# One product taken out of a mixing stage: second half of the conditioning, fetched by GpSimd in other stages

## What is computed

```python
mod = silu(c) @ w_ada + b_ada                       # (2048) x (2048, 6*2048)
sh1, sc1, g1, sh2, sc2, g2 = split(mod, 6)
u   = rms_norm(x) * (1 + sc1) + sh1
xa, ya, xb, xc, gl = split(u @ w_in)                # LRU, gelu gate, pool, Fourier, branch gates
lru_out  = ((h_f + h_b) * gelu(ya)) @ w_lru_out     # two scans over the tokens, gates from xa
pool_out = multiscale_pool(xb) @ w_pool * pool_scale
four_out = real(fft2(xc)) @ w_fourier
x = x + g1 * ((g_lru*lru_out + g_pool*pool_out + g_four*four_out) @ w_out)
v = rms_norm(x) * (1 + sc2) + sh2
x = x + g2 * ((silu(v @ w_gate) * (v @ w_up)) @ w_ffn_out)
out = rms_norm(x)
```

## Time and profile before

| | |
|---|---|
| median of three runs | 2697.18 us (2695.38 to 2698.59) |
| the profiled execution, its time | 2696.47 us |
| its span | 2694.7 us |
| mean granted TensorE clock | 0.992 |
| TensorE busy | 2660.4 us (99%) |
| VectorE busy | 1585.1 us (59%) |
| ScalarE busy | 1016.1 us (38%) |
| GpSimd busy | 69.8 us (3%) |
| mean DMA rate | 180 GB/s |

### The profile page before, as it was taken

One profiled execution on the slowest core, in us unless ns is written; L12 is line 12 of the kernel. 1 busy time (PEld: TensorE's weight loads), 2 busy tenths in 40 slices (PEclk: granted clock), 3 DMA queues, 4 the chain that ended last, 5 costly groups with the idle time before them and its releaser, 6 DMA issues.

```text
span 2694.7 us, 35961 instructions
## 1 busy us (share of the span) xinstructions
PE 2660.4 (99%) x13497; PEld 2223.4 (83%) x13497; DVE 1585.1 (59%) x1740; ACT 1016.1 (38%) x1138; POOL 69.8 (3%) x84
## 2 busy tenths in 40 slices
PE   7999999999999999999999999999999999999998
PEld 5788778888888888888788888888888888888887
DVE  5525878654555544633568878878787763343443
ACT  4214675222222222322335444444444442242333
POOL 0000000000000000000001000001010000000000
PEclk8999999999999999999999999999999999999999
DMA  9922223565556665644368888878888844544555
GB/s 366 362 72 86 90 86 105 189 202 187 191 189 195 196 194 177 189 145 140 102 178 202 211 196 203 202 200 201 199 202 196 211 138 156 182 157 163 184 175 192
DMA packets 443200, 485.88 MB, mean 180 GB/s; under 512 B 14904, under 2 KB 388992, under 8 KB 438016
## 3 DMA queue, kind: packets, MB, share of 16 engines
q1 hardware_dynamic: 411504, 371.57, 44.0%
q0 software_dynamic: 11520, 41.95, 8.8%
q10 hardware_dynamic: 20112, 71.48, 8.5%
HBM read 418.88 MB, written 24.12 MB: 164 GB/s over the span
## 4 chain that ended last, share of the span: by engine, by line
PE 97%; DMA 1%; DVE 1%; ACT 1%; ACTq 0%; issue 0%; SPq 0%; DVEq 0%
PE main L1033 15%; PE main L1034 15%; PE main L1035 15%; PE main L1361 10%; PE aux L1361 10%; PE main L1365 5%; PE aux L1365 5%; PE aux L1410 4%; PE aux L1411 4%; PE aux L1412 4%; PE main L1410 1%; PE main L1411 1%; PE main L1412 1%; PE aux L1199 1%; PE aux L1085 1%; DMA ada_pc<-in_w_ada 1%
## 5 line engine op out<-in xcount | busy, mean ns | idle before, releaser
L1033 PE MATMUL main<-u_both,w_hi 128*128 128x512 f32 x1536 | 611.1, 398 | 2.5 <-DVE u_both L1886 2.5
L1034 PE MATMUL main<-u_both,w_hi 128*128 128x512 f32 x1536 | 599.8, 390 | 0.0
L1035 PE MATMUL main<-u_both,w_lo 128*128 128x512 f32 x1536 | 598.7, 390 | 0.0
L1527 DVE TENSOR_TENSOR w_lo<-w_raw,w_hi 128x1024 fp32r<-128x1024 f32 x216 | 263.0, 1223 | 448.8 <-ACT w_hi L607 448.2
L607 ACT ACTIVATE w_hi<-w_raw 128x1024 fp32r<-128x1024 f32 x216 | 227.5, 1056 | 508.4 <-DMA w_raw<-in_w_in 314.1
L1033 PEld LDWEIGHTS main<-u_both,w_hi 128*128 128x128 f32 x1536 | 289.3, 188 | 75.3 <-issue 19.3
L1035 PEld LDWEIGHTS main<-u_both,w_lo 128*128 128x128 f32 x1536 | 289.1, 188 | 61.5
L1034 PEld LDWEIGHTS main<-u_both,w_hi 128*128 128x128 f32 x1536 | 289.3, 188 | 58.0 <-issue 4.1
L879 ACT ACTIVATE h_S<-f_S 128x1024 fp32r<-128x1024 f32 x160 | 165.3, 1057 | 228.7 <-DVE f_S L1929 95.4
L2032 DVE TENSOR_TENSOR hb_l<-hb_f,hb_h 128x2048 fp32r<-128x2048 f32 x33 | 75.7, 2292 | 256.6 <-ACT hb_h L941 256.6
L1410 PE MATMUL aux<-hb_h,bw_h 128*128 128x512 f32 x512 | 200.0, 391 | 0.9 <-DVE bw_l L2037 0.9
(11 more groups left out here) (274 smaller groups left out, 3966.4 us busy)
## 6 DMA issues: line engine op xcount, KB each, us to landing
w_raw<-in_w_in SPq DMA_DIRECT2D x144, 512.0 KB, 3.6
ada_pc<-in_w_ada ACTq DMA_DIRECT2D x128, 512.0 KB, 4.3
f_A<-in_w_ffn_in SPq DMA_DIRECT2D x120, 512.0 KB, 5.3
bw_f<-in_w_ffn_out SPq DMA_DIRECT2D x88, 512.0 KB, 6.8
f_S<-in_w_ffn_in SPq DMA_DIRECT2D x80, 512.0 KB, 4.2
f_S<-f_A POOLq DMA_DIRECT2D x80, 512.0 KB, 5.7
hb_f<-hidden_feature_major SPq DMA_DIRECT2D x33, 1024.0 KB, 4.9
ada_pc<-in_w_ada SPq DMA_DIRECT2D x48, 512.0 KB, 7.3
```

Of the source, the lines that this page charges most:

```text
L1033: pe.matmul(dst, wh, m_hi_ap, start=start, stop=False, skip_group_check=shared)
L1034: pe.matmul(dst, wh, m_lo_ap, start=False, stop=False, skip_group_check=shared)
L1035: return pe.matmul(dst, wl, m_hi_ap, start=False, stop=stop, skip_group_check=shared)
L1527: dve.tensor_tensor(w_lo[:, s], w_raw[:, s], w_hi[:, s].bitcast(F32), ALU.subtract).then_inc(lo_done, 1)
```

## The change

The 128 pieces leave the mixing stage, and their DMAs leave ScalarE's queue for GpSimd's. Blocks 0 and 1 (pieces 0 to 31) run in stage 2: twelve pieces between `lo(0, 8, 0, 9)` and `xa_out(0, 0)`, the others after the `lo` steps of units 8 to 15. They come through four buffers that lie where x_raw was; GpSimd starts them when x_raw has been stored and u formed. Block 2 runs in the eight gate windows, two pieces in each. Blocks 3 to 5 run in the first three iterations of the output projection. Blocks 6 and 7, which are g2 and needed last, are taken together in pieces of 1 MB during the first pass of the down projection. The one-column matmuls follow: a group of eight behind units 9 and 15, one in the first mixing iteration, one in each of the output iterations 1 to 3, and one of sixteen in the last group of the first down pass. mod2 is made in four parts, and second_modulation moves to the last output iteration. Two small buffers change their place, and a second set of m_lo waits is left out.

The constants and buffers:

```diff
+EARLY_CHUNKS = {8: (12, 13, 14, 15), 10: (16, 17), 11: (18, 19), 12: (20, 21, 22), 13: (23, 24, 25), 14: (26, 27, 28), 15: (29, 30, 31)}
+OUT_CHUNKS = {1: (0, 1), 2: (2, 3, 4), 3: (5, 6), 4: (7, 8, 9), 5: (10, 11, 12), 6: (13, 14, 15)}
+LATE_AT = 96
...
-        ada2_pc = sb("ada2_pc", "ada", [2, 1024])
+        ada2_pa = sb("ada2_pa", "yx", [4, 1024])
+        ada2_pc = sb("ada2_pc", "pf", [2, 1024])
+        ada2_pw = sb("ada2_pw", "lru", [4, 1024])
+        ada2_pl = sb("ada2_pl", "lru", [2, 2, 1024], F32, 16 * kb)
+        ada2_al = sb("ada2_al", "ada", [2, 1024])
```

GpSimd:

```diff
+            def chunk(n, dst):
+
+                i, cc = n // 16, n % 16
+                pool.dma_start(dst, ada_t[:, cc, 2 * D + 1024 * i:2 * D + 1024 * i + 1024]).then_inc(ada2_landed[n % 4], 16)
+
+            pool.wait_ge(x_stored, 16)
+            pool.wait_ge(u_aff, 2 * KT)
+            for n in range(32):
+                if n >= 4:
+                    pool.wait_ge(ada2_used, n - 3)
+                chunk(n, ada2_pa[:, n % 4, :])
+            for n in range(32, 48):
+                pool.wait_ge(ada2_used, n - 1)
+                chunk(n, ada2_pc[:, n % 2, :])
+            pool.wait_ge(unit_used, G_OUT)
+            for n in range(48, 96):
+                pool.wait_ge(ada2_used, n - 3)
+                chunk(n, ada2_pw[:, n % 4, :])
...
+            pool.wait_ge(product_done, 7 * NWIN)
+            for m in range(16):
+                if m >= 2:
+                    pool.wait_ge(ada2_used, LATE_AT + 2 * m - 2)
+                src = ada_t[:, m, 5 * D:6 * D].rearrange("p (a n) -> p a n", a=2)
+                pool.dma_start(ada2_pl[:, m % 2, :, :], src).then_inc(ada2_landed[m % 2], 16)
```

TensorE:

```diff
+            def spread(i):
+
+                pe.wait_ge(ada2_used, i * 16 + 16)
+                for t in range(8):
+                    ins = pe.matmul(aux[:, 2, ds(i * 8 + t, 1)], ada2_acc[:, t * P:t * P + P], ones[:, 0:1], start=True, stop=True)
+                ins.then_inc(acc_used, 1)
...
+                    if u in (9, 15):
+                        spread((9, 15).index(u))
...
-                pe.wait_ge(ada2_used[1], i * 8 + 8)
-                for t in range(8):
-                    ins = pe.matmul(aux[:, 0, ds(i * 8 + t, 1)], ada2_acc[:, t * P:t * P + P], ones[:, 0:1], start=True, stop=True)
-                ins.then_inc(acc_used, 1)
...
-                        pe.wait_ge(m_lo, UC * k + UC)
+                        if first and j == 0:
+                            pe.wait_ge(m_lo, UC * k + UC)
                         unit(G_OUT, 8, i, 4 * j + k, j, u_of(k), k == 0, k == 3, half_done if last and j and k == 3 else None)
+                        if not first and j == 0 and k == 0:
+                            spread(i + 2)
...
+                        if ps == 0 and u == 0:
+                            pe.wait_ge(ada2_used, LATE_AT + 32)
+                            for t in range(16):
+                                ins = pe.matmul(main[:, 2, t:t + 1], ada2_al[:, t // 8, (t % 8) * P:(t % 8) * P + P], ones[:, 0:1],
+                                                start=True, stop=True)
```

VectorE (the third block stands in each gate window, the fourth behind the steps of an output iteration, the last in the down groups of the first pass):

```diff
+            def chunk(src, n, k, first=False):
+
+                if first:
+                    ins = dve.tensor_scalar(ada2_acc[:, :], src, cvec[:, k, 0:1], None, ALU.mult)
+                else:
+                    dve.wait_ge(ada2_used, n)
+                    ins = dve.scalar_tensor_tensor(ada2_acc[:, :], src, k, ada2_acc[:, :], ALU.mult, ALU.add)
+                ins.then_inc(ada2_used, 1)
...
             lo(0, 8, 0, 8)
             lo(0, 8, 0, 9)
+            chunks_early(*range(12))
             xa_out(0, 0)
             xa_out(0, 1)
             for u in range(8, 16):
                 lo(0, 8, 0, u + 2)
+                chunks_early(*EARLY_CHUNKS.get(u, ()))
...
+                    if u == 1:
+                        for q in range(2):
+                            dve.wait_ge(ada2_landed[2 * p + q], hh * 16 + 144)
...
+                    for cc in () if last else OUT_CHUNKS.get(u, ()):
+                        dve.wait_ge(ada2_landed[cc % 4], i * 64 + (13 + cc // 4) * 16)
...
                     prep(gg % 2, nu, splits_before(gg))
+                    if ps == 0:
+                        chunks_late(0, 2 * g - 4)
+                        chunks_late(0, 2 * g - 3)
...
+                if ps == 0:
+                    dve.wait_ge(acc_used, 7)
+                    dve.tensor_tensor(mod2[:, 48:64], main[:, 2, 0:16], prm[:, C_BADA + 80:C_BADA + 96], ALU.add).then_inc(mod2_done, 1)
```

More of the change, by code:

```diff
@@ L250, in build @@
         dft_landed = sem("dft_landed")
-        ada2_landed = [sem(f"ada2_landed{s}") for s in range(2)]
+        ada2_landed = [sem(f"ada2_landed{s}") for s in range(4)]
         res_landed = [sem(f"res_landed{s}") for s in range(2)]
@@ L797, in _ @@
             chunk_out(2)
-            ada2(0, 2)
             hi(G_MIX, 16, 0, 7)
             chunk_out(3)
-            for u in (3, 4, 5):
-                ada2(0, u)
             for g in range(4):
@@ L1257, in mix @@
                             u += 1
+                            if first and j == 0 and k == 0:
+                                pe.wait_ge(tanh_done, 16)
+                                spread(2)
                         if first and j == 0:
@@ L1285, in _, with out_proj @@
                 mix(i)
-            def out_proj(i, last=False):
+            def out_proj(i, first=False, last=False):
                 for j in range(2):
@@ L1291, in out_proj @@
                     for k in range(4):
-                        pe.wait_ge(m_lo, UC * k + UC)
+                        if first and j == 0:
+                            pe.wait_ge(m_lo, UC * k + UC)
                         unit(G_OUT, 8, i, 4 * j + k, j, u_of(k), k == 0, k == 3, half_done if last and j and k == 3 else None)
-            with pe.Fori(0, 3) as i:
+                        if not first and j == 0 and k == 0:
+                            spread(i + 2)
+            out_proj(0, first=True)
+            with pe.Fori(1, 3) as i:
                 out_proj(i)
-            out_proj(3, True)
+            out_proj(3, last=True)
             pe.wait_ge(sq_added, 6)
@@ L1695, in product_lo, with window @@
                 dve.tensor_tensor(act_r[:, ds(h, 1), 1, :], act_f[:, ds(h, 1), 1, :], act_r[:, ds(h, 1), 0, :].bitcast(F32), ALU.subtract).then_inc(act_lo, 1)
-            def window(h, base, per, i, u0, first=False, last=False):
+            def window(h, hh, p, base, per, i, u0, first=False, last=False):
                 for u in range(4):
@@ L1702, in window @@
                         final(h - 1)
+                    if u == 1:
+                        for q in range(2):
+                            dve.wait_ge(ada2_landed[2 * p + q], hh * 16 + 144)
+                            if first and q == 0:
+                                dve.wait_ge(acc_used, 2)
+                                chunk(ada2_pc[:, q, :], 32, 0, True)
+                            else:
+                                chunk(ada2_pc[:, q, :], h * 2 + (32 + q), cvec[:, ds(h * 2 + q, 1), 0:1].rearrange("p o n -> p (o n)"))
                     if u == 2 and not first:
@@ L1714, in _ @@
                 dve.wait_ge(ctx_free[j], 2)
+            mod2_out(0, 2)
             conv(0)
-            window(0, G_YX, 4, 0, 0, first=True)
+            window(0, 0, 0, G_YX, 4, 0, 0, first=True)
             with dve.Fori(0, 3) as i:
                 chain.enter(i, 0, 22)
-                window(i * 2 + 1, G_YX + 4, 8, i, 0)
-                window(i * 2 + 2, G_YX + 4, 8, i, 4)
+                window(i * 2 + 1, i, 1, G_YX + 4, 8, i, 0)
+                window(i * 2 + 2, i + 1, 0, G_YX + 4, 8, i, 4)
                 chain.leave(3)
-            window(7, G_YX + 28, 4, 0, 0, last=True)
+            window(7, 3, 1, G_YX + 28, 4, 0, 0, last=True)
             def pool_group(g):
@@ L1849, in out_steps @@
                             mixed_lo(k)
-                    if first and u == 1:
+                    if last and u == 1:
                         second_modulation()
@@ L2085, in fin_evac, with chunks_late @@
                                 main[:, 2, :].rearrange("p (t f) -> p t f", f=P)).then_inc(fin_out_v, 1)
+            def chunks_late(i, m):
+                q = m % 2
+                dve.wait_ge(ada2_landed[q], i * 32 + 16 * (25 + m // 2))
+                for t in range(2):
+                    if isinstance(i, int) and m == 0:
+                        ins = dve.tensor_scalar(ada2_al[:, t, :], ada2_pl[:, q, t, :], cvec[:, 0, 0:1], None, ALU.mult)
+                    else:
+                        dve.wait_ge(ada2_used, i * 8 + (LATE_AT + 2 * m + t - 1))
+                        k = cvec[:, ds(i * 4 + m, 1), 0:1].rearrange("p o n -> p (o n)")
+                        ins = dve.scalar_tensor_tensor(ada2_al[:, t, :], ada2_pl[:, q, t, :], k, ada2_al[:, t, :], ALU.mult, ALU.add)
+                    ins.then_inc(ada2_used, 1)
             for ps, nu in enumerate((3, 3, 2)):
```

62 lines of the change are left out of this document (26 added, 36 removed).

## The result

The changed kernel takes **2716.88 us** (median of 4 executions, 2714.09 to 2719.48) against 2696.28 before (4 executions beside it): ratio 1.0075, 95% interval 1.0057 to 1.0092. The forecast was 2705.8, range 2702.0 to 2713.5. The direction was right; the forecast size was 2.4 times too small (+20.6 instead of +8.6), and the time lies outside the range.

What follows compares the result with a forecast made beforehand. TensorE, busy 99% of the span, was taken to bound the kernel, so relieving other engines buys nothing. Late start 7.0 + half clock 1.6 + 0 = +8.6 us on the median 2697.18 gave 2705.8; range 2702 to 2713.5.

Steps and rivals of the forecast that it cites:

- the removal at 0: Mixing stage: eight one-column groups leave TensorE, 14.7 us off, balanced by the same products added elsewhere; the rest was hidden.
- rival (d): Mixing stage: not slower, as 2880 matmul pitches shorten when the pieces leave; up to -11.6 us, 2685.6; chance 0.03.
- The stop of TensorE at unit 8, 7.0 us: State projection: the copy that frees unit 8's buffer stands behind twelve pieces, so TensorE starts 7.0 us late; bounds 6.0 to 14.6.
- the landing at 4.6 us with regular arrival: Early pieces on GpSimd's queue: each lands 4.6 us after issue, plus 0.1 for the signal; bounds 3.5 and 8.4.
- VectorE's own pace, 1.38 a piece: Early pieces in the state projection: dependent pieces follow each other on VectorE at a step of 1.38 us.
- Half clock behind the stop, 1.6: Unit 8's first matmuls: TensorE's clock falls to its lower level after the stop, costing 1.6 us; bounds 0 and 3.4.
- The group of sixteen, 0 with a bound of +1.7: First down pass: sixteen one-column products cost twice 1.84, 3.7 us, with no net loss; +1.7 if the clock falls there.
- Gate windows, output projection, down pass, 0: Later stages: the moved pieces fit into VectorE's waits and spare time, 0 us; down pass bound 7 groups at 1 us.
- Rival (b): Down pass: late pieces make it wait 1 us in seven groups; +15.6 us in all, 2712.8; chance 0.08.
- (a): State projection: GpSimd's queue is slower, landing at 8.4 us or fewer than four pieces in flight; +16.2, 2713.4; chance 0.14.
- (c): State projection: the stop is short and the clock holds, only VectorE's 1.28 a piece counting; 4.9 us, 2702.1; chance 0.10.
- (e): State projection: the early copy doesn't wait for the pieces, so nothing moves; 2697; chance 0.05.

Runs made afterwards that it cites:

- the order experiment: Changed kernel with only VectorE's order altered, the two context copies ahead of the pieces, and TensorE's first early group behind unit 11: 2699.43 us, ratio 1.0013.
- the hold: Changed kernel with one more wait in GpSimd's list, third and later pieces held until unit 9's weight tile has landed and been rounded: 2713.66 us.
- the three split versions: Late sixteen products split into two eights: changed kernel, 2716.72 us; with copies ahead of pieces and VectorE's wait moved, 2694.56 us, and again 2695.28 us.

## Why the prediction was wrong

- **What bounds the kernel, and the removal at 0**: right. Busy time within 1.1 us, iterations 1.87 us shorter, no wait gone; rival (d) (shorter pitches) is out.
- **The stop of TensorE at unit 8, 7.0 us**: right in place and cause (the order experiment takes it away), wrong in size, 15.4 late. This is the step that failed, by two terms of the path to VectorE's copy.
- First, "Before, lo(9) ends at 140.86" was carried over as the start of the pieces. That is a time from a trace in which the DMA engines carried nothing but the two tiles then. The 2 MB that GpSimd asks for at that very moment put unit 9's tile off, for which the sum had no term: **+6.15 us** of the stop (5.4 in two other traces). I had priced what the tile's traffic does to the pieces (the landing) but not what the pieces' does to the tile, although the tile stands ahead of all twelve in VectorE's list.
- Second, the landing at 4.6 us with regular arrival: 1 us of waits forecast, 3.1 measured, **+2.2 us** (1.8 and 2.7 in the two others). The median landing between 133 and 166 us is 5.1.
- **VectorE's own pace, 1.38 a piece**: right, 1.39 measured.
- **Half clock behind the stop, 1.6**: right in kind, too small. It cost 2.1 here for fourteen matmuls, and 1.35 to 2.9 over the seven traces with a stop; eight matmuls at the norm were one draw of a number that varies.
- **The group of sixteen, 0 with a bound of +1.7**: the clock fell in six of seven traces, for 1.7 us (the bound) in three and 2.5 to 2.7 (over the bound) in three.
- **Gate windows, output projection, down pass, 0**: right; no new wait. Rival (b) is out.
- **Rivals (a) and (b), (c), (e)**: (a) came nearest, +16.2, but mostly by another mechanism: the landings explain 2.2 us, the tile 6.15. Its "fewer than four in flight" would have made the stop shorter at the tile and longer at the pieces, as the hold shows. (c) and (e) are out, as the stop came and the clock fell in it.
- **The range**: it took in the bounds of the landing (14.6) and of the late clock one at a time; no bound stood for the tile, which I had not seen as a term.
- "I am wrong if ... its size is set by landings over 5 us" came true, by the tile's landing of 9.9.
- **Two slips that change nothing**: 0.86 in the window from 1314 puts the fall of the clock at 1314.7, not 1314.9, and -20 + 8.6 is -11.4, not -11.6.

## What to carry to other kernels

When a change puts new transfers beside old ones, list the old transfers that are in flight at that moment and who waits for each, and price their delay: here 1.2 to 1.7 us for each 512 KB in flight. Being asked for first didn't help the tile, as the queues took turns by packet and the other queue's were four times as large. Look in an in-order engine's list for anything urgent behind work that can be late: the same 16 us of VectorE's work on pieces stopped nobody behind the copies and made a stop of 15 us ahead of them, and a wait that moved by one unit cost 1.6. And count from an instruction behind the noisy start, not from zero: it made 2 us visible where the times spread by 5.

## What the hardware showed that I had not expected

- A plain load of 512 KB on GpSimd's queue landed in 3.7, 5.6 and 9.0 us (least, median, most of 96 in the changed kernel), much like the adding ones of the earlier trace rows (4.6, 5.7, 8.4). The Trainium skill's 2.0 us plus bytes over 436 GB/s (DMA: Bandwidth & Descriptors, Anatomy of one DMA — SWDGE (gpsimd) path), an estimated 3.2 us, is below the least of them.
- GpSimd issues such a load in 0.53 us when its rows are 4 KB; with 1 KB rows it takes 0.75 us, and the next follows 3.4 to 4.8 us later, held by nothing that the profile shows. Both kinds go in 143 to 144 packets a piece, so four rows of 1 KB share a packet of 4 KB, while the weight tiles on SyncE's queue, also in rows of 1 KB, have one packet a row (1,057 packets for two tiles, before).
- Two queues with work got about as many packets each from the DMA engines (431 and 453 in 5 us), not as many bytes.
- Sixteen one-column fp32 products in a row (3.63 us) were followed by a fall of the clock in six traces of seven; the groups of eight in the down pass of the three split versions were not. At the lower clock level eight take 3.41 us instead of 1.84.
